# Small expert items: both sets of turning sums move behind two chunks, ahead of the low products of their pair

## What is computed

```python
top_val, top_idx = lax.top_k(logits, TOP_K)          # 4 of 32 experts per token
gates = jax.nn.softmax(top_val, axis=-1)
hgu = lax.ragged_dot(xs, w_gate_up, group_sizes) + b_gate_up[e_sorted]   # 1024 -> 2048
x_glu = jnp.minimum(hgu[..., ::2], 7.0)
x_lin = jnp.clip(hgu[..., 1::2], -7.0, 7.0)
act = x_glu * jax.nn.sigmoid(1.702 * x_glu) * (x_lin + 1.0)
out = lax.ragged_dot(act, w_down, group_sizes) + b_down[e_sorted]        # 1024 -> 1024
```

## Time and profile before

| what | value |
|---|---|
| median of three runs | 1978.24 us (1969.84 to 1981.0) |
| the profiled execution | 1977.72 us, of which the span is 1976.0 us |
| TensorE (PE) busy | 1860.8 us, 94% |
| VectorE (DVE) busy | 1647.7 us, 83% |
| ScalarE (ACT) busy | 1356.4 us, 69% |
| PE idle ahead of the turning sums (line 1177) | 42.8 us in 36 places |

### The profile page before, as it was taken

The page is one execution under the profiler, slowest core; times in us unless marked ns, Lnnn a source line. Parts: engine busy times, 40 slices in busy tenths (PEclk is TensorE's granted clock), DMA queues, the critical chain, the costliest instruction groups (busy, mean ns, idle before and its releaser), DMA issues.

```text
span 1976.0 us, 28564 instructions
## 1 busy us (share of the span) xinstructions
PE 1860.8 (94%) x8378; PEld 1462.4 (74%) x8378; DVE 1647.7 (83%) x1766; ACT 1356.4 (69%) x1777; POOL 479.6 (24%) x412
## 2 busy tenths in 40 slices
PE   6999999998989998999999999999899999999897
PEld 3657767787768886787777787777777778778775
DVE  6899987359765478989889888998888998999988
ACT  4556855224345526888778887888878888888885
POOL 6671000000000117312422322342222222222132
PEclk7999999999999988999989999999999999999989
DMA  8222225423010258999999999999999999999995
GB/s 321 77 107 86 86 90 178 139 82 100 22 43 23 65 179 245 366 382 375 363 372 384 373 357 380 374 374 379 363 368 390 364 371 363 383 384 356 393 390 207
DMA packets 134431, 526.20 MB, mean 266 GB/s; under 512 B 15809, under 2 KB 21089, under 8 KB 114208
## 3 DMA queue, kind: packets, MB, share of 16 engines
q1 hardware_dynamic: 118704, 492.45, 66.4%
q0 software_dynamic: 15664, 32.97, 6.3%
HBM read 512.76 MB, written 23.74 MB: 272 GB/s over the span
## 4 chain that ended last, share of the span: by engine, by line
PE 38%; DMA 7%; ACT 7%; issue 5%; DVE 5%; ACTq 0%; SPq 0%; DVEq 0%
PE ps L1128 32%; DMA ring<-in_w_gate_up 4%; PE ps L1177 4%; DVE split L2818 3%; ACT arena_r L2016 2%; ACT split L2016 2%; PE ps L1083 2%; DMA arena<-in_w_gate_up 2%; ACT arena L2041 1%; PE ps L1167 1%; DVE arena_r L2818 1%; DMA arena<-in_w_down 1%; DVE ring L2949 0%; DVE small L2942 0%; ACT arena L2052 0%
## 5 line engine op out<-in xcount | busy, mean ns | idle before, releaser
L1128 PE MATMUL ps<-split,xTs 128*128 128x512 f32 x2016 | 506.4, 399 | 20.0 <-DVE split L2818 14.6
L1128 PEld LDWEIGHTS ps<-split,xTs 128*128 128x128 f32 x2016 | 379.2, 191 | 116.8 <-DVE split L2818 30.6
L2818 DVE TENSOR_TENSOR split<-ring,split 128x2048 fp32r<-128x2048 f32 x136 | 308.1, 2295 | 26.4 <-ACT split L2016 20.8
L2818 DVE TENSOR_TENSOR split<-arena,split 128x2048 fp32r<-128x2048 f32 x136 | 308.5, 2287 | 1.9 <-ACT split L2016 1.8
L2016 ACT ACTIVATE split<-ring 128x1024 fp32r<-128x1024 f32 x272 | 271.7, 1057 | 38.7 <-DMA ring<-in_w_gate_up 24.4
L2016 ACT ACTIVATE split<-arena 128x1024 fp32r<-128x1024 f32 x272 | 270.6, 1053 | 24.4 <-DMA arena<-in_w_down 6.3
L839 POOL DMA_INDIRECT y_rows<-arena,slots x50 | 121.7, 2434 | 325.1 <-issue 282.9
L1128 PE MATMUL ps<-arena_r,xTs 128*128 128x512 f32 x672 | 181.7, 405 | 0.3
L1128 PE MATMUL ps<-arena_r,aTs 128*128 128x512 f32 x672 | 178.8, 413 | 0.0
L2016 ACT ACTIVATE arena_r<-arena 128x1024 fp32r<-128x1024 f32 x136 | 141.8, 1059 | 36.6 <-PE ps L1128 20.3
L1128 PE MATMUL ps<-split,aTs 128*128 128x512 f32 x672 | 164.8, 394 | 0.4
(11 more groups left out here) (478 smaller groups left out, 3105.5 us busy)
## 6 DMA issues: line engine op xcount, KB each, us to landing
ring<-in_w_gate_up SPq DMA_DIRECT2D x170, 1024.0 KB
arena<-in_w_gate_up SPq DMA_DIRECT2D x102, 1024.0 KB
arena<-in_w_down SPq DMA_DIRECT2D x102, 1024.0 KB
ring<-in_w_down SPq DMA_DIRECT2D x34, 1024.0 KB
ring<-in_w_in SPq DMA_DIRECT2D x23, 1024.0 KB
ring<-in_w_out SPq DMA_DIRECT2D x8, 1024.0 KB
ring<-in_mod_w SPq DMA_DIRECT2D x10, 512.0 KB, 9.1
ring<-in_mod_w SPq DMA_DIRECT2D x4, 1024.0 KB
```

Source lines behind the costliest of these rows:

```text
L1128: m = mm(ps[:, banks + q, :], lhs[:, x_, k, :], w[:, q * 512:(q + 1) * 512], start=start, stop=stop)
L2818: V.tensor_tensor(split_pair(1, p), chunk_pair(p), split_pair(0, p), ALU.subtract).then_inc(sig("lo_ready"), 1)
```

## The change

Both turning sums of a small item move. `turn_sum(0)` comes after both chunks of pair 4 instead of after the first. `turn_sum(1)` goes into pair 8, behind its two chunks and ahead of its low products, and `turn_next` follows the whole of pair 8; so the waits for `y_ready` and for `at_lo` of the first half now stand ahead of `turn_sum(1)`. Big items are as before. No instruction is added or removed, and ScalarE, VectorE, GpSimd and SyncE keep their order.

```diff
-                    def down(p, within=None):
-
-                        pair(p, 4, aTs, p // 2 * 4 - 16 + p % 2, p == 8, p == 11, within, None)
+                    def down(p, within=None, between=None):
+
+                        pair(p, 4, aTs, p // 2 * 4 - 16 + p % 2, p == 8, p == 11, within, between)
...
-                        up(4, lambda: turn_sum(0))
+                        up(4, None, lambda: turn_sum(0))
                         up(5)
                         up(6, None, lambda: bias(1))
                         up(7)
-                        turn_sum(1)
-                        turn_next()
                         pe.wait_ge(sig("y_ready"), i + 0)
                         pe.wait_ge(sig("at_lo"), i * 2 + 3)
-                        down(8)
+                        down(8, None, lambda: turn_sum(1))
+                        turn_next()
                         down(9)
```

## The result

The changed kernel takes **2002.87 us** (median of 4 runs, 1989.95 to 2011.36) against 1979.62 us for the kernel before (4 runs). The ratio is 1.0115, with a 95% interval of 1.0085 to 1.0146: it is slower by 23 us. The forecast was 1966 us, within 1949 to 1989 us, so the sign is wrong and the range is missed. The profiled execution took 2011.36 us, with a span of 2009.7 us, and is the slowest of the four. So what follows leans on single places and single stretches, not on its total.

A forecast was written before the change was run, and what follows sets the result against it. The prediction took TensorE to set the pace from a small item's second turning sums on, a tile in transit before that. From the profiled execution, 1977.7 + 13 - 25 + 0 = 1966 us, range 1949 to 1989 us.

The forecast's parts named there:

- What bounds the kernel: From a small item's second turning sums TensorE sets the pace; its lost microseconds there are paid nearly in full.
- The second place: The second half's turning sums, around pairs 7 and 8 of a small item, where `turn_sum(1)` and `turn_next` move.
- the first place: The first half's turning sums, at pair 4 of a small item, where `turn_sum(0)` moves.
- turning sums 0: First half, pair 4: time won is waited out for VectorE in front of low products 7; costed at 0.
- Turning sums 1: Second half: waiting 1.49 us for `at_lo` delays the sums 1.0 us and pair 10 0.9 us; +13 us.
- The clock, -25 us: Around pairs 7 and 8: matmuls between wait and sums keep TensorE's clock up, saving 0.85 steps an item.
- steps: Pieces of about 3.4 us at 1.2 instead of 2.4 GHz on TensorE; 22 in 13 stretches, 1.7 per small item.
- the two weak places: Wait, pair 7, wait, which stays; and second wait with thin sums and `turn_next` behind, which was to go.
- the first rival: The clock falls as often as before, leaving the 13 us of late activation; slower, 1991 us, chance 15%.
- The price of a step: Each 3.4 us low-clock piece on TensorE lengthens a stretch (one small plus one big item) by 1.64 us.
- The signs: Expected profile: idle before turning sums under 15 us, new 1.5 us wait for `at_lo`, up to 0.9 before pair 10, quicker stretches.
- The fourth: Sign that stretches between small items would mostly be at clock 0.98 or above and take 70 us or less.

The follow-up runs named there:

- e1_first_only: Kernel before with only the first half's turning sums moved behind both chunks of pair 4; 1982.23 us, ratio 1.0019.
- e11_second_early: `e3_early_at_lo` with the first half's turning sums put back behind one chunk of pair 4; 1959.97 us, ratio 0.9897.
- e5_after_fill: Changed kernel plus five additional matmuls with unused result behind pair 7, in the wait for `at_lo`; 1969.81 us, ratio 0.9941.
- e3_early_at_lo: Changed kernel, but VectorE writes `at_lo` of the first half one split earlier, ahead of the low part of pair 8; 1955.79 us, ratio 0.9882.
- e2_second_only: Kernel before with only the second half's turning sums and the turning of the next rows moved; 1993.53 us, ratio 1.0066.
- e4_before_fill: Kernel before plus four additional matmuls with unused result behind pair 7, ahead of the second turning sums; 1969.32 us, ratio 0.9950.
- e7_next_inside: Changed kernel with `turn_next` right behind the second turning sums, ahead of the low products of pair 8; 1988.98 us, ratio 1.0050.

## Why the prediction was wrong

*What bounds the kernel: right.* The second place and the path behind it decide; `e1_first_only` and `e11_second_early` leave the first place within a few us. My 0 for *turning sums 0* stands to within 4 us, with opposite signs in the two.

*Turning sums 1, +13 us: right.* The wait of 1.49 us is there with 1.62, the 0.9 us before pair 10 with 0.95, and the term measures 14 us twice (`e5_after_fill` against `e3_early_at_lo`, and `e2_second_only` against the kernel before at the same clock). Its working is less exact than its result: 11.3, 0.6 and nothing make 12, not 13, and the new wait stands in all 18 small items, not in 15. The wait before pair 10 is there in full only where the clock holds: 6.4 us in all in the changed kernel, 17.0 us in `e5_after_fill`.

***The clock, -25 us: this step failed, in its sign.*** I expected 0.85 steps an item instead of 1.7. Read like the earlier trace rows, the 14 stretches of the changed kernel hold 30 steps, 2.1 an item. By the mean clock over all runs (0.958 in eight runs of the changed kernel, 0.961 in those of the kernel before) that is some 16 us more at 1.2 GHz, where the prediction had 52 us less. With 2002.9 - 1979.6 = 23 us in all and 14 from the delay, about +9 us are left for the clock's term; it is a difference, not a measurement of its own. I argued that one of the two weak places goes when four matmuls come between the wait and the sums. They do come between, but in 13 of 18 places the clock is down before or among them. The place that I let stand, wait, four matmuls, wait, is where it mostly starts, and then it lasts longer: nine falls of 10 us or more behind 830 us, where the kernel before has one. Here is one fall of each kernel in 14 us of TensorE, first before, then after; the means of 0.76 and 0.63 say 6.7 and 10.4 us at 1.2 GHz:

```profile
1558.00:1572.00 14.00, 12.43 (x53) 0.76 1.02 406
...
1579.00:1593.00 14.00, 12.56 (x49) 0.63 0.98 380
```

In the changed kernel it covers pair 8's chunks, sums, low products and turning. Why it lasts longer there, and why it stays away in five items, some with waits just like those of items in which it comes, no run shows. I had named the outcome, in the first rival ("with pair 8 inside it; four matmuls at 1.2 GHz then even delay the sums"), priced only the delay, and gave it 15%. The kernel came out at 2003 us where that rival said 1991 us, and its price lacked the longer low clock.

*The price of a step, 1.64 us: too high for gains.* Between the profiled executions of the change and of `e5_after_fill` the mean clock rises from 0.954 to 0.983, that is from 2 x 0.046 x 2010 = 185 us at 1.2 GHz to 2 x 0.017 x 1967 = 67 us. The 118 us fewer bring 2011.4 - 1968.2 = 43 us, 0.37 us for each (by the medians and the clocks over all runs it is 33 us for 98, or 0.34), where the earlier trace rows gave 1.64 for 3.4, or 0.48. In the kernel before, `e4_before_fill` got 0.19. The same hide the reason: no stretch there is at 1.00. In the changed kernel those at 1.00 take 69.6 to 69.9 us, no less than the ones at 0.98 before. There something else sets the pace, and in this kernel the late sums have a part in it: with them the stretches of `e5_after_fill` above take 69.3 us, without them those of `e3_early_at_lo` at the same place 68.1 to 68.5 us. What paces the kernel before there is not shown.

*The signs.* The three on waits came as named (9.0 us before the sums, 1.62 us before pair 8, 0.95 us before pair 10). The fourth did not: four stretches of 14 are at 0.98 or above, and three take 70 us or less.

*The Trainium skill.* The rule that I weighed against the change ("TensorE: Matmul & The Clock Gate", on a second HAM failure mode), that short idles between groups of matmuls keep the clock switching, agrees with the traces better than my estimate did: with waits of 1.68 and 1.43 us around four matmuls the clock fell. It does not say when: with 1.22 and 1.62 us it held once, with 1.23 and 1.62 us it fell.

*The chance was real.* With the cause of the wait removed, the same order on TensorE gains 21 us, at a clock of 0.980 instead of 0.961. I had put down 25 us for the clock. That the two are so near is in part luck: some 76 us less at 1.2 GHz are behind the 21 us, where I had 52 us at a higher price, and what the filled wait for the copy gives is in them too.

## What to carry to other kernels

A step that is moved ahead in one engine's order brings its waits with it: look up when each of its signals really comes, in all instances, also signals for which nobody waits today. Where such a signal is late by its producer's order, move the producer first; here one line on VectorE turned a loss of 1.15% into a gain of 1.2%. And a price read from two levels of a resource holds between these levels; before a gain is extrapolated to the end, some row has to show what takes over there. Last, where single runs scatter, set the means over all runs side by side: a single profile of each would make the clock look like the cause in `e7_next_inside`.

## What the hardware showed

Work without a use can be worth its time: five matmuls of 512 columns in a wait of 1.6 us in each small item made the changed kernel 33 us faster, with the mean clock up from 0.958 to 0.982. The granted clock fell at places where no wait was longer than 1.7 us, and then stayed at 1.2 GHz over the whole sequence: 16 products took 3.51 us instead of 1.90. The same pair of waits (1.2 and 1.6 us) once brought the fall and once did not. DMA engines that are 0.99 to 1.02 busy were no sign of a bound: the stretches shown at that share took from 68.1 to 73.3 us.
